# Moving the sum of the last layer norm's gate from layer 1's mixer into the last expert

## The reference

```python
c_act = jax.nn.silu(c)
for l in range(DEPTH):
    mod = (c_act @ w_mod[l] + b_mod[l])[:, None, :]
    sh1, sc1, g1, sh2, sc2, g2 = jnp.split(mod, 6, axis=-1)
    h = x * (1.0 + sc1) + sh1
    y = hybrid_mixer(h, ...)
    x = layer_norm(DN_ALPHA * x + (1.0 + g1) * y, ln_g[l, 0], ln_b[l, 0])
    h = x * (1.0 + sc2) + sh2
    y = swiglu(h, ...) if l % 2 == 0 else moe_swiglu(h, ...)
    x = layer_norm(DN_ALPHA * x + (1.0 + g2) * y, ln_g[l, 1], ln_b[l, 1])
```

## Time and profile before

| | us |
|---|---|
| median of 3 runs (lowest, highest) | 1275.26 (1275.22, 1275.42) |
| profiled execution, its own time | 1272.66 |
| its span | 1270.9 |
| first product of the experts starts | 528.15 |
| last down product ends | 1253.0 |
| mean granted TensorE clock | 0.983 of full |

### The profile page before, as it was taken

How to read it: one execution, slowest core, us unless ns; L and a number is a source line. 1 busy time by engine, 2 the same in 40 slices (tenths; PEclk the granted TensorE clock), 3 DMA queues, 4 the chain that set the end, 5 groups by cost and what they waited for, 6 DMA issues and landing times.

```text
span 1270.9 us, 26228 instructions
## 1 busy us (share of the span) xinstructions
PE 1183.0 (93%) x11180; PEld 641.1 (50%) x11180; DVE 569.0 (45%) x913; ACT 302.1 (24%) x521; POOL 43.8 (3%) x84
## 2 busy tenths in 40 slices
PE   1889889999999898799999999999999999999996
PEld 1879867788878787523334323334233233333332
DVE  6799988677758999421021020111210210210224
ACT  0557243433336571310010010100100100100100
POOL 2101010000011010000000000000000000000001
PEclk9899989999999999799999999999999999999998
DMA  9973868899727648889999989999989999999950
GB/s 340 312 257 116 290 227 312 322 347 329 244 68 239 201 167 315 334 326 371 413 364 414 394 299 414 412 364 411 388 310 411 410 364 404 396 362 411 379 233 34
DMA packets 149083, 403.60 MB, mean 318 GB/s; under 512 B 19964, under 2 KB 71328, under 8 KB 137696
## 3 DMA queue, kind: packets, MB, share of 16 engines
q1 hardware_dynamic: 146720, 395.16, 82.5%
q0 software_dynamic: 2240, 6.68, 1.4%
HBM read 400.75 MB, written 1.05 MB: 316 GB/s over the span
## 4 chain that ended last, share of the span: by engine, by line
PE 75%; DVE 13%; DMA 6%; issue 3%; ACT 2%; SPq 1%; POOL 0%; DVEq 0%; ACTq 0%
PE bank L1349 36%; PE bank L1368 18%; PE bank L337 5%; PE bank L339 4%; PE bank L338 4%; DVE mod_acc L1541 3%; DMA raw_u<-in_ffn_w_up_dram 2%; DMA u_raw<-in_w_in_dram 2%; DVE u_low L1552 2%; PE bank L1331 1%; DMA mod_first<-in_w_mod_dram 1%; PE bank L1228 1%; DVE score L1596 1%; PE bank L1339 1%; PE bank L1022 1%
## 5 line engine op out<-in xcount | busy, mean ns | idle before, releaser
L1349 PE MATMUL bank<-raw_w,xg 128*32 128x512 f32 (+1 forms) x4608 | 462.9, 557 | 4.5 <-issue 2.5
L1349 PEld LDWEIGHTS bank<-raw_w,xg 128*32 128x32 f32 x4608 | 147.1, 110 | 304.7 <-issue 304.6
L1368 PE MATMUL bank<-raw_w,heT 128*32 128x512 f32 x2112 | 232.9, 593 | 0.0
L1915 DVE TENSOR_TENSOR he<-he,bank 128x256 f32<-128x256 f32 (+1 forms) x72 | 25.6, 384 | 369.4 <-ACT he L869 369.4
L869 ACT ACTIVATE he<-bank 128x256 f32<-128x256 f32 (+1 forms) x72 | 21.2, 367 | 542.8 <-PE bank L1349 542.8
L1368 PEld LDWEIGHTS bank<-raw_w,heT 128*32 128x32 f32 x2112 | 67.3, 110 | 150.5 <-issue 149.3
L1942 DVE SCALAR_TENSOR_TENSOR ycat<-bank,gate_tab,ycat 128x512 f32<-128x512 f32 x36 | 25.4, 747 | 173.0 <-PE bank L1340 171.1
L1541 DVE SCALAR_TENSOR_TENSOR mod_acc<-mod_row,c_act,mod_acc 128x1024 f32<-128x1024 f32 x70 | 89.8, 1283 | 6.8 <-DVE mod_acc L1541 0.9
L337 PE MATMUL bank<-u_high,hT_H 128*128 128x256 f32 x256 | 75.4, 294 | 4.9 <-DVE u_low L1552 3.5
L339 PE MATMUL bank<-u_high,hT_L 128*128 128x256 f32 x256 | 72.8, 284 | 0.0
L338 PE MATMUL bank<-u_low,hT_H 128*128 128x256 f32 x256 | 72.6, 284 | 0.0
(11 more groups left out here) (284 smaller groups left out, 1378.7 us busy)
## 6 DMA issues: line engine op xcount, KB each, us to landing
raw_w<-in_moe_w_down_dram SPq DMA_DIRECT2D x88, 1024.0 KB, 8.6
raw_w<-in_moe_w_gate_dram SPq DMA_DIRECT2D x128, 512.0 KB, 8.5
raw_w<-in_moe_w_up_dram SPq DMA_DIRECT2D x128, 512.0 KB, 9.8
mod_row<-in_w_mod_dram SPq DMA_DIRECT2D x80, 512.0 KB, 6.4
raw_w<-in_moe_w_gate_dram SPq DMA_DIRECT2D x64, 384.0 KB, 5.6
raw_w<-in_moe_w_up_dram SPq DMA_DIRECT2D x64, 384.0 KB, 6.8
u_raw<-in_w_in_dram SPq DMA_DIRECT2D x20, 1024.0 KB, 7.5
raw_d<-in_ffn_w_down_dram SPq DMA_DIRECT2D x11, 1024.0 KB, 10.1
```

Of the source, the lines that this page charges most:

```text
L1349: last = mm(bank[g][32 * q:32 * q + 32, 0:2 * HALF[c]].rearrange("s (m j r) -> s m j r", m=2, r=64), xg[:, i, k, 32 * g:32 * g + 32], cols ...
L1368: last = mm(bank[3 + g][32 * q:32 * q + 32, :], heT[(par + c) % 2][:, g, 2 * a + b, :], W[:, b, h * 512:(h + 1) * 512], start=(c == 0 and ...
L1915: V.tensor_tensor(h, h, bank[g][:, w:2 * w].rearrange("s (j c b) -> s j b c", b=2, c=32), ALU.mult).then_inc(s["m_hid"], 1)
```

## The change

The gate `g2` of layer 1 leaves the list of conditioning parts, with its eight rows, its place in the mixer on SP, VectorE and TensorE, and the wait between the transposes of tile 0 and 1. In the last expert four loads of 1 MB (two rows each) follow the last down load in ring slots whose tiles have been used. VectorE sums rows 0 to 3 into a new tile `gate3_acc` ahead of the last hidden chunk and rows 4 to 7 behind it, both ahead of `last_G`. TensorE multiplies the sum by a new matrix of ones (`ones_late`; the hidden values have overwritten the old one) behind the transposes of `last_G` and in front of the last down products. The application and the two waits for it move behind.

```diff
-MODS = [(0, 2), (0, 3), (0, 4), (1, 0), (1, 1), (1, 3), (1, 4), (0, 5), (1, 2), (1, 5)]
+MODS = [(0, 2), (0, 3), (0, 4), (1, 0), (1, 1), (1, 3), (1, 4), (0, 5), (1, 2)]
...
+        gate3_acc = place("gate3_acc", [P, D], at=over + 42 * 1024)
+        ones_late = place("ones_late", [P, P], at=hidT_at + 8192 + 3072)
...
-                               {5: (64, 65), 8: (66, 67), 9: (68, 69, 70, 71), 15: (72, 73)})
+                               {5: (64, 65), 8: (66, 67), 9: (68, 69, 70, 71)})
...
-            load_mod_rows(*range(74, len(MOD_ROWS)))
...
-            sp.wait_ge(s["yT_L"], 8)
+            sp.wait_ge(s["row_rd"], len(MOD_ROWS))
...
             pair_loads(last, n_last, None)
+            for i in range(4):
+                n = PER_PAIR - KT + i
+                slot_free(n_last, n)
+                sp.dma_start(raw_w[(FIRST + n) % NRAW][:], w_mod[1, 2 * i * P:2 * (i + 1) * P, 5 * D:6 * D].rearrange("(j p) d -> p j d", p=P))\
+                    .then_inc(g_ld[i], 16)
...
+            act_expert(n_last, 1, True, True)
             act.wait_ge(s["modT"], 11)
-            act_expert(n_last, 1, True, True)
...
-                        elif l and t and i == 2:
-                            pe.wait_ge(s["row_rd"], len(MOD_ROWS))
-                            gate_sum(11, (0, 3))
...
             transposed_tile(3, 0)
-            pe.wait_ge(s["modT"], 11)
             transposed_tile(3, 1)
...
                         last.then_inc(s["m_st"], 1)
+                        pe.wait_ge(s["m_hid"], E * 9 + 9)
+                        pe.wait_ge(s["g_rows"], 1)
+                        for h in range(2):
+                            last = mm(bank[h][:], ones_late[:], gate3_acc[:, h * 512:(h + 1) * 512], start=True, stop=True)
+                        last.then_inc(s["mod_ps"], 1)
...
-                if ph == 2:
-                    gate_apply(11, (0, 3), gate3_row)
...
-                condition_rows(range(72, 76) if l else range(12, 16))
+                if l == 0:
+                    condition_rows(range(12, 16))
                 gate_apply(10 if l else 2, (1, 2), g_row)
                 low_unit(l, NIN + 3)
-                condition_rows(range(76, 80) if l else range(16, 24))
                 if l == 0:
+                    condition_rows(range(16, 24))
...
+            def gate_rows(rows):
+                for k in rows:
+                    dve.wait_ge(g_ld[k // 2], 16)
+                    row = raw_w[(FIRST + PER_PAIR - KT + k // 2) % NRAW][:, k % 2, :]
+                    if k == 0:
+                        last = V.tensor_scalar(gate3_acc[:], row, c_act[:, 0:1], None, ALU.mult)
+                    else:
+                        last = V.scalar_tensor_tensor(out=gate3_acc[:], in0=row, scalar=c_act[:, k:k + 1], in1=gate3_acc[:],
+                                                      op0=ALU.mult, op1=ALU.add)
+                    if k < KT - 1:
+                        link(last)
+                    else:
+                        last.then_inc(s["g_rows"], 1)
...
+                if ends:
+                    V.memset(ones_late[:], 1.0)
+                    gate_rows(range(0, 4))
                 hidden_chunk(pr, par, 2)
-                if not ends:
+                if ends:
+                    gate_rows(range(4, KT))
+                else:
                     hidden_chunk(pr, par, 3)
...
             dve.wait_ge(s["m_acc"], n_done * 4 + 4)
+            gate_apply(11, (0, 1), gate3_row)
+            dve.wait_ge(s["modT"], 11)
```

More of the change, by code:

```diff
@@ L97 @@
            + (HF + YC) * 10
-           + YC + HF + [YC0, X0 + 6, X0 + 4, X0 + 5] + HF + [X0 + i for i in range(4)] + HF)
+           + YC + HF + [YC0, X0 + 6, X0 + 4, X0 + 5])
 PT_BANK = (6, 7, 0, 1, 3, 0)
@@ L304, in hybrid_decoder @@
             rt_ps lg8 expd sel rank_ps npass lg_rd xb_ps xsplit xsplitL G xg_ps xg
-            m_used m_silu m_hid m_tH m_oS m_st m_S m_sc m_acc m_y0 m_y1 m_yH m_yL m_end""".split():
+            m_used m_silu m_hid m_tH m_oS m_st m_S m_sc m_acc m_y0 m_y1 m_yH m_yL m_end g_rows""".split():
             s[name] = sem("s_" + name)
@@ L311, in hybrid_decoder @@
         m_ld = [sem(f"s_m_ld{i}") for i in range(NRAW)]
+        g_ld = [sem(f"s_g_ld{i}") for i in range(4)]
         block = ctx.enter_context(nc.Block())
@@ L394, in load_mod_rows @@
                         sp.wait_ge(s["proj"], mix * NU + U_KEYS + 1)
-                    if n in (12, 72):
-                        sp.wait_ge(s["pv_ps"], 2 * mix + 2)
+                    if n == 12:
+                        sp.wait_ge(s["pv_ps"], 2)
                     if n in (9, 69):
@@ L400, in load_mod_rows @@
                         sp.wait_ge(s["pv_ps"], 2)
-                    if n == 74:
-                        sp.wait_ge(s["yT_L"], 8)
                     if n == ROWS_DENSE:
```

## The result

| | before | after |
|---|---|---|
| median of 18 runs (lowest, highest), us | 1275.22 (1273.31, 1277.58) | 1278.88 (1275.55, 1283.80) |
| ratio, 95% interval | | 1.0032 (1.0021 to 1.0042) |
| profiled execution, us | 1272.66 | 1280.37 |

The change makes the kernel 0.3% slower, 3.7 us; the forecast was 1274.7 and no measurable change. What two executions say of a cause has to be held against more of them, which the experiments supply.

The account below looks back on a forecast made before the run. TensorE's expert stage was taken as the bound, with VectorE mostly on the critical chain in the tail before it. Terms -2.45 + 1.71 + 0.2 = -0.5 us gave 1274.7 us, no measurable change; range 1272.0 to 1277.2.

Parts of the forecast that it names:

- The tail's gain of 2.45 us: Tail of layer 1's mixer: without the gate's row sums and two matmuls, the experts start 2.45 us earlier.
- the last expert's cost of 1.7: Last expert on TensorE: two added f32 matmuls before the last down products, uncovered, cost 1.71 us.
- the second load's landing at 1233.1: Last expert: the second added 1 MB load lands at about 1233.1 us, at 2.5 us per MB.
- the one-hot's margin of 0.2 us: Last expert: VectorE finishes the last one-hot at 1244.1 us, TensorE asks for it at 1244.27.
- The term of 0.2: Last expert: 0.2 us of TensorE stall for the last one-hot, taken between no stall and 1 us.
- The Trainium skill's 4.4 us for 1 MB: Added loads: 2.0 us plus bytes over 436 GB/s; by it no stall and a sum 0.2 us lower.
- the code's placement: Rival: two loop edges idle 1.3 and 1.2 us without releaser; moved code may add or remove 1.3 us; no chance given.
- An earlier start carries through to the end one for one: Expert stage, some 725 us of TensorE work: any earlier start shortens the whole kernel by as much.
- The clock rival: Rival around the router: TensorE's clock differs, 5.3 us gain at most or 1.2 us loss; 10% for gain past 0.2%.
- VectorE becomes the bound: Rival, last expert: late rows stall TensorE at the last one-hot, 2.6 us, 1277.1; 20% slower than before, 6% past 0.2%.
- the tail gives nothing back: Rival, mixer's tail: a wait of the same length replaces the removed work, +1.9 us, 1277.2; 5%.
- all of the 10.6 us are gained: Rival, mixer's tail: VectorE alone is the bound, so all removed row-sum time is gained, 1266.6 us; 3%.

Follow-up runs that it names:

- the changed kernel again: The changed kernel with no edit, run and profiled a second time: 1278.59 us, ratio 1.0026 to the kernel before.
- with 2, 29 and 61 transposes: Changed kernel plus that many idle identity transposes before TensorE's 13.9 us wait for the first sums; single executions 1280.98, 1270.35 and 1276.53 us.
- 10 ahead: TensorE's loop stands ten instructions earlier in the code than in the kernel before, as in the unpadded changed kernel: 1278.59 us, ratio 1.0026.
- 48 behind: Loop 48 instructions later than in the kernel before, by idle transposes: kernel before with 24, 1270.91 us (0.9974); changed kernel with 29, 1272.09 us (0.9976).
- 10 and 6 ahead: Changed kernel's loop ten or six instructions earlier than in the kernel before, without and with two idle transposes: 1278.59 us, and 1280.98 us in one execution.
- 0 and 16 behind: Loop where the kernel before has it, or 16 instructions later; changed kernel with five idle transposes 1274.18 us, with 13 1276.86 us in one execution.
- the old place: Loop where the kernel before has it: that kernel 1274.95 us; changed kernel with five idle transposes 1274.18 us (0.9992).
- 118 behind: Loop 118 instructions later than in the kernel before, by idle transposes: kernel before with 59, 1276.08 us (1.0009); changed kernel with 64, 1277.19 us (1.0020).

## Why the prediction was wrong

**The work in the two edited places: right.** The tail's gain of 2.45 us was measured as 2.4 to 2.6 (column a, and the distance to tile 1's statistics); the last expert's cost of 1.7 as 1.8; the second load's landing at 1233.1 as 1233.6 on that scale; the one-hot's margin of 0.2 us was 0.10, and in four of the later profiles (the changed kernel again and with 2, 29 and 61 transposes) TensorE waited for it by 0.2 to 0.6 us. The term of 0.2 was the right size. TensorE's waits, the changed kernel again:

```profile
PE bank L1422 <- DVE last_G L1999: 0.4, 1, 0.4
```

The Trainium skill's 4.4 us for 1 MB, which the prediction set beside its row, comes from a section on DMAs of the GpSimd path. These four loads are SP's and took 10.0 us each at the median, so the sum was right to go by the row.

**The step that failed is the last rival, "the code's placement"**, which stood in the range with "1.3 us each way" and had no term in the sum, no chance and no mechanism. It cost 3.1 to 3.7 us of column d: edges of 3.9 to 4.5 us in place of 2.5, and half clock behind one of the two edges (1.7 us) in each of the three profiles with the loop 10 ahead (3.9 - 2.5 + 1.7 = 3.1, 4.5 - 2.5 + 1.7 = 3.7). Over all profiles, of the eight edges with waits of 1.82 to 2.51 us three were followed by half clock, and of the fourteen with waits up to 1.33 us none. The forecast had treated the rows with no releaser as noise of unknown sign. They are a cost of the place, and by the packets' rows each is a wait for instructions that begin to load too late for the edge: 1.19 to 1.33 us at the old one in three kernels, 1.86 to 2.06 at 10 ahead but for one of 2.51, none at 48 behind in three profiles. The forecast had also leaned on three runs of the kernel before that spread by 0.2 us; its 18 runs spread by 4.3.

The Trainium skill says in "Runtime: NRT & Kernel Launch", section "Instruction fetch mechanics", that each engine's instructions are fetched in order in blocks of 16 KiB, and that a taken branch to a target outside the blocks at hand has to fetch it first. The traces agree with the size of the packets and with the waits' end behind one. They do not show that a stall must come: with the loop 48 instructions behind, the packet began early enough and TensorE never waited, on a loop whose edge is hinted to the engine in the code (`hint_back_edge`). Which instructions a packet holds no trace shows, nor why it begins in steps (alike at 10 and 6 ahead, alike at 0 and 16 behind).

**"An earlier start carries through to the end one for one" was not shown either.** The first expert product was to start 2.45 us earlier, and under 1.5 us was named as a sign of being wrong. Counted from gate 10's sum it starts 40.09 us behind in the changed kernel and 41.34 before, 1.25 us earlier (1.65 on the average of all profiles, columns a and b): the gathers at 1.2 GHz took the rest.

**The clock rival was half right.** It was given 10% and only for a gain; the price of slow gathers, 1.2 us, was worked out and is what column b shows. The chunk of expert 0 behind the 2.0 us wait, with 1.7 us at stake, was not seen: in the profile of before it ran at full clock, and nothing in those rows said that it could be otherwise. Here the Trainium skill's rule that the gate's windows run free of the kernel ("TensorE: Matmul & The Clock Gate", "What's actually happening") agrees with what the two executions of the same kernel show, 5.29 and 6.99 us in column c.

**The net of the change at equal place** is -0.8 (at the old place), +1.2 (48 behind) and +1.1 us (118 behind) by the medians of the table; by the ratios it is -0.0008, +0.0002 and +0.0011, of 1275 us -1.0, +0.3 and +1.4, each with an interval of over 1 us either way. The forecast of -0.5 us lies among them, and so does the sum of the columns' means, -2.4 + 0.7 + 0.9 + 1.8 = +1.0. The last pair, at 118 behind, was to tell 0.5 to 1 us faster from 1 us or more slower; its medians say slower, but within their intervals they do not decide. By the profiles the clock decides: with c at full clock in both kernels the columns add up to 761.34 us in the changed kernel against 762.33 before at 118 behind, and 757.69 against 758.29 at 48 behind, the forecast's gain; the other profile at 48 behind, with slow gathers and a slow chunk, adds up to 760.50. Whether the new tail makes the low clock likelier is left open. So is which property of the place sets when the packet begins; seven places were tried and no rule was found. Of the rivals, "VectorE becomes the bound" fell (0.6 us of stall at most, where 0.75 was to decide the sign), and so did "the tail gives nothing back" and "all of the 10.6 us are gained" (column a).

## What to carry to other kernels

Ten instructions more or less ahead of a TensorE loop can be worth more than the edit that moved them: before an edit of under 1% is judged, look at the waits without a releaser at the loop's back edges and at the instruction packets in front of them, and time the edited kernel with the loop put back where it stood (idle instructions in a stretch where the engine waits anyway). If the edges are long, try a few places: here one of seven took both waits away, worth 0.25%. When a wait on TensorE grows towards 2 us, count the half clock behind it as well as the wait.

## What the runs showed of the hardware that was not expected

- A loop edge costs TensorE from 0 to 2.5 us by where the loop stands in the code. At one place it repeats from kernel to kernel within 0.2 us, but for one of 2.51 us where five others gave 1.86 to 2.06.
- The profile can show such an edge as a wait of 1.04 us 20 records into the loop while 2.1 us are lost.
- Instruction loads stand in the trace as packets of 16 KB. TensorE went on 2.4 to 2.9 us after one began in all 22 waits at or just behind the edges, and did not wait where one had begun 3.2 us or more ahead (6 edges).
- A wait of 2.04 us for the hidden values is followed by 1.7 us of lost clock in 9 of 14 profiles, and a wait of 1.82 to 2.51 us at an edge in 3 of 8 edges; none of the 14 edges with a shown wait of 1.33 us or less was. (9 of 14 profiles are column c's.)
